# A two-part transformer forward pass on one core: another order of tiles in the mixing stage, earlier loads, squares one tile later

## The reference

```python
f = swiglu(rmsnorm(x, g1), w_gate, w_up, w_down);  x = x + 0.5 * rmsnorm(f, g2)
h = rmsnorm(x, mix_pre_g)
qa, ka, va, qb, kb, vb, gate_a, gate_b = split(h @ w_in)
ya = neighbourhood_attention(qa, ka, va, rpb) @ w_branch_a   # 8 heads, 8 rows x 16 columns, bias from rpb
yb = dilated_mixture(qb, kb, vb) @ w_branch_b
x = x + rmsnorm((sigmoid(gate_a) * ya + sigmoid(gate_b) * yb) @ w_out, g3)
...
# end of each hybrid layer: the per-layer embedding p, gated
x = x + sigmoid(rmsnorm(x, ple_g) @ w_ple_gate) * (p @ w_ple_proj)
# rope tables of the layers: cos and sin of positions * inv_freq
```

## Time and profile before

| | |
|---|---|
| median of 3 runs | 3201.22 us (3196.33 to 3205.59) |
| the profiled execution | 3208.67 us, its span 3206.9 us |
| mean granted TensorE clock | 0.988 |
| TensorE (PE) busy | 3094.5 us, 96% |
| VectorE (DVE) busy | 1714.4 us, 53% |
| ScalarE (ACT) busy | 1203.8 us, 38% |
| GpSimd (POOL) busy | 294.1 us, 9% |
| mean of one: L1705 cast, L1831 split, L1867 diagonal | 983, 1167, 689 ns |
| L1948 (mask), x6 | 1220 ns each |

### The profile page before, as it was taken

How to read it: one execution, slowest core, us unless ns; L and a number is a source line. 1 busy time by engine, 2 the same in 40 slices (tenths; PEclk the granted TensorE clock), 3 DMA queues, 4 the chain that set the end, 5 groups by cost and what they waited for, 6 DMA issues and landing times.

```text
span 3206.9 us, 40495 instructions
## 1 busy us (share of the span) xinstructions
PE 3094.5 (96%) x15386; PEld 2513.3 (78%) x15386; DVE 1714.4 (53%) x3078; ACT 1203.8 (38%) x2229; POOL 294.1 (9%) x351
## 2 busy tenths in 40 slices
PE   7999989999999999999999999999999999999997
PEld 5888777788788887777768888887877767888886
DVE  5653355346565426656656555435656665555435
ACT  3332325433433223645543323223545453332222
POOL 2000110001100012011001100012111001100002
PEclk9999999999999999999999999999999999999999
DMA  4323373225322333224216222333323314323332
GB/s 143 117 92 113 111 134 117 79 93 178 102 92 93 99 115 97 82 90 157 70 40 191 99 99 92 97 113 117 95 82 114 126 44 151 122 94 104 96 96 92
DMA packets 107569, 339.65 MB, mean 106 GB/s; under 512 B 16608, under 2 KB 17136, under 8 KB 107248
## 3 DMA queue, kind: packets, MB, share of 16 engines
q1 hardware_dynamic: 86384, 273.90, 26.9%
q0 software_dynamic: 20992, 63.15, 6.6%
HBM read 300.55 MB, written 27.52 MB: 102 GB/s over the span
## 4 chain that ended last, share of the span: by engine, by line
PE 83%; DVE 5%; ACT 5%; issue 3%; DMA 2%; POOL 1%; SPq 0%; POOLq 0%; DVEq 0%; ACTq 0%
PE bk L1537 24%; PE bk L1539 24%; PE bk L1538 24%; PE bk L1602 2%; PE bk L1624 2%; ACT t L1757 2%; PE bk L1610 2%; PE bk L1574 1%; PE bk L1576 1%; PE bk L1575 1%; ACT t L1705 1%; ACT t L1765 1%; DVE t L1831 1%; PE bk L1592 0%; PE bk L1587 0%
## 5 line engine op out<-in xcount | busy, mean ns | idle before, releaser
L1537 PE MATMUL bk<-t,t 128*128 128x512 f32 x3808 | 1499.1, 394 | 41.6 <-DVE t L1831 21.4
L1539 PE MATMUL bk<-t,t 128*128 128x512 f32 x3808 | 1482.3, 389 | 0.0
L1538 PE MATMUL bk<-t,t 128*128 128x512 f32 x3808 | 1481.3, 389 | 0.0
L1537 PEld LDWEIGHTS bk<-t,t 128*128 128x128 f32 x3808 | 719.6, 189 | 210.0 <-issue 51.2
L1831 DVE TENSOR_TENSOR t<-t,t 128x1024 fp32r<-128x1024 f32 (+3 forms) x540 | 620.3, 1167 | 421.1 <-ACT t L1705 420.6
L1538 PEld LDWEIGHTS bk<-t,t 128*128 128x128 f32 x3808 | 720.2, 189 | 147.6 <-issue 3.6
L1539 PEld LDWEIGHTS bk<-t,t 128*128 128x128 f32 x3808 | 719.4, 189 | 148.6
L1705 ACT CAST t<-t 128x1024 fp32r<-128x1024 f32 (+3 forms) x540 | 515.3, 983 | 227.8 <-PE bk L1539 116.3
L1757 ACT ACTIVATE t<-t,t 128x256 f32<-128x256 f32 (+3 forms) x336 | 174.1, 520 | 143.0 <-DVE t L1908 142.2
L1748 ACT CAST t<-t 128x512 fp32r<-128x512 f32 x88 | 54.7, 622 | 435.6 <-DVE t L1895 435.6
L2138 POOL TENSOR_TENSOR t<-t,t 128x512 f32<-128x512 f32 x65 | 86.9, 1337 | 1424.4 <-ACT t L1735 1423.6
(11 more groups left out here) (165 smaller groups left out, 2045.7 us busy)
## 6 DMA issues: line engine op xcount, KB each, us to landing
t<-in_f_g SPq DMA_DIRECT2D x88, 512.0 KB, 4.3
t<-in_f_u SPq DMA_DIRECT2D x88, 512.0 KB, 3.5
t<-in_f_d SPq DMA_DIRECT2D x64, 512.0 KB, 4.4
t<-in_gate SPq DMA_DIRECT2D x48, 512.0 KB, 3.7
gate_scratch<-t POOLq DMA_DIRECT2D x64, 256.0 KB, 2.3
t<-gate_scratch POOLq DMA_DIRECT2D x64, 256.0 KB, 3.9
t<-in_f_d SPq DMA_DIRECT2D x32, 384.0 KB, 3.2
t<-in_wo SPq DMA_DIRECT2D x24, 512.0 KB, 3.6
```

The costliest lines, as they stand in the source:

```text
L1537: pe.matmul(o, wh, xh, start=start, stop=False)
L1538: pe.matmul(o, wh, xl, start=False, stop=False)
L1539: return pe.matmul(o, wl, xh, start=False, stop=stop)
```

## The change

In the mixing stage the table loads wait for `ft[7]`, the last stored tile of the feed-forward, instead of `fr`. The q tiles come first and as one `dense4`, then three k tiles, the masks of heads 0 to 3, the values with their store and loads, the masks of heads 4 to 7, and the last k tile. The load of the positions is planned before `bias_tables`. In the embedding each tile's square is planned after the next tile's `dense`; in layer 0 the first three chunks are gained before the last tile's `gate`, the other five after it, and the last square after these.

```diff
--- before.py
+++ after.py
@@ -704,27 +704,32 @@
         va = [tile([128, 2, T], RA + (32 + 4 * w + 24 * (w > 1)) * K) for w in range(4)]
         BT = tile([128, 3, 8, 256], RA + 40 * K)
         bt_w = [self.load(BT[16 * r:16 * r + 16].rearrange("p w h k -> p (w h) k"),
-                          D["tables"][:, :, :, 7 - r:15 - r, :].rearrange("c w h a k -> c (w h) (a k)"), self.tables_t, fr)
+                          D["tables"][:, :, :, 7 - r:15 - r, :].rearrange("c w h a k -> c (w h) (a k)"), self.tables_t, ft[7])
                 for r in range(8)]
-        v_n = self.tokens_first("va", 512, 2, H, lambda t: vn[:, t, :], fr, by=lambda: (self.nv, self.nv_tok))
-        vst = self.load(D["values"].rearrange("(t p) c -> p t c", p=128), vn[:], v_n)
-        v_t = [[self.load(va[w][:, j, :],
-                          bass.AP(D["values"].tensor, (256 * j + WINDOWS[w]) * T, [[64 * T, 4], [T, 32], [1, T]]), fr, vst)
-                for j in range(2)] for w in range(4)]
         qt_, kt_ = [], []
         bt_ = {}
 
         def by_columns(a):
             return a.rearrange("p (r t c) -> p t r c", r=8, t=4)
 
+        for m, r in enumerate(self.dense4([("qka", m) for m in range(4)], H)):
+            qt_.append(self.evacuate(OB, *r, qa[:, m, :].rearrange("p (t r c) -> p t r c", t=4, r=8), fr, view=by_columns))
+        def masks(h0):
+            for kind in range(3):
+                n = self.step("biased", bt=BT[:, kind, h0:h0 + 4, :], window=kind, t=bt_w)
+                for i in range(h0, h0 + 4):
+                    bt_.setdefault(i, []).append((n, "d"))
+
         for m in range(4):
-            qt_.append(self.project("qka", m, H, qa[:, m, :].rearrange("p (t r c) -> p t r c", t=4, r=8), fr, view=by_columns))
-        for m in range(4):
+            if m == 3:
+                masks(0)
+                v_n = self.tokens_first("va", 512, 2, H, lambda t: vn[:, t, :], fr, by=lambda: (self.nv, self.nv_tok))
+                vst = self.load(D["values"].rearrange("(t p) c -> p t c", p=128), vn[:], v_n)
+                v_t = [[self.load(va[w][:, j, :],
+                                  bass.AP(D["values"].tensor, (256 * j + WINDOWS[w]) * T, [[64 * T, 4], [T, 32], [1, T]]),
+                                  fr, vst) for j in range(2)] for w in range(4)]
+                masks(4)
             kt_.append(self.project("qka", 4 + m, H, ka[:, m, :], fr))
-            for kind in range(3) if m % 2 == 0 else ():
-                n = self.step("biased", bt=BT[:, kind, 2 * m:2 * m + 4, :], window=kind, t=bt_w)
-                for i in range(2 * m, 2 * m + 4):
-                    bt_.setdefault(i, []).append((n, "d"))
         ob4 = {}
         oa_t = []
         na_us = []
@@ -913,8 +918,8 @@
         ki = tile([128, T], RA + 72 * K, I32)
         kf = tile([128, T], RA + 74 * K)
         r = [tile([128, T], RA + (76 + 2 * i) * K) for i in range(4)]
+        a = self.load(pi_[:], D["positions"].partition_broadcast(128), self.now())
         self.bias_tables()
-        a = self.load(pi_[:], D["positions"].partition_broadcast(128), self.now())
         yield
         done = []
         x = None
@@ -1444,7 +1449,12 @@
         fr = self.now()
         if L == 0:
             fetch, halves, product, store = self.embed(1, 4, RA, RA + 8 * K, fr, raw_at=RA + 16 * K)
-        new, back = [], {}
+        new, back, due, ht = [], {}, [], []
+
+        def squares():
+            for f in due:
+                f()
+            due.clear()
 
         def bring(m):
             if m < KC:
@@ -1459,8 +1469,12 @@
             tmp.give(io, (k, "o"))
             n = self.step("ple", m=m, s=s, t=[(k, "o"), xt[m]])
             tmp.give(i, (n, "d"))
-            self.acc_tok, r = self.square_in(self.xT[:, m, :], m == 0, (n, "d"), on="dve" if m == KC - 1 else "pool")
-            new.append([(n, "d"), r])
+            new.append([(n, "d")])
+
+            def square():
+                self.acc_tok, r = self.square_in(self.xT[:, m, :], m == 0, (n, "d"), on="dve" if m == KC - 1 else "pool")
+                new[m].append(r)
+            due.append(square)
 
         bring(0)
         bring(1)
@@ -1471,17 +1485,21 @@
                 fetch()
             if L == 0 and m == 5:
                 halves()
+            squares()
             if L == 0 and m == KC - 1:
                 for j in range(4):
                     product(j)
+                ht = [self.gained(9, c, list(new[c]), tg) for c in range(3)]
             if self.factor_due:
                 self.late.append(lambda a=(m, bg, gb, tg): gate(*a))
             else:
                 gate(m, bg, gb, tg)
         xt = new
-        ht = []
+        if L == 1:
+            squares()
         if L == 0:
-            ht = [self.gained(9, c, xt[c], tg) for c in range(KC)]
+            ht += [self.gained(9, c, list(xt[c]), tg) for c in range(3, KC)]
+            squares()
             xt = [[a, b] for a, b in zip(xt, ht)]
             for j in range(4):
                 store(j)
```

## The result

| | before | after |
|---|---|---|
| median | 3203.4 us (3196.33 to 3206.79, 4 runs) | 3166.58 us (3163.22 to 3167.88, 4 runs) |
| ratio, 95% interval | | 0.9882 [0.9871, 0.9893] |
| the profiled execution | 3208.67 us, span 3206.9 | 3163.22 us, span 3161.4 |
| mean granted TensorE clock | 0.988 | 0.996 |

A forecast was written before the change was run, and what follows sets the result against it. TensorE, busy 96%, bounds the kernel; only standing still and lower-clock stretches can go. 12.0 + 9.6 + 9.9 + 0.6 = 32.1 us off 3208.67 gives 3176.6; against the median 3201.22, 3169.1, range 3159 to 3186.

The forecast's parts named there:

- Positions: First feed-forward: the positions' load goes out sooner, VectorE's splits are done by 46.6, TensorE's stall goes; gain 12.0 us.
- the clock's share of it: First feed-forward: the lower clock behind the 9.07 us stall cost a further 2.9 us, part of the 12.0.
- Mixing: Mixing stage: q tiles first and tables earlier bring the first scores to 470.0 instead of 479.60; gain 9.6 us.
- a new wait of 3.9 us takes the place of the 8.28: Norm's second matmul (L1592): weights start when tables end, land at 433.3, so it cannot start before 436.5.
- The rival of shared queues: Mixing stage: the weight load shares engines from issue, the wait is 1 us, time 3166; chance 0.12.
- Values: Attention's first slot: value loads landed by E + 20.8, wanted at E + 22.3 (E: value tokens' end); cost 0.
- the rival of late values: Attention's first two slots wait as store or small loads meet weight loads; up to 18.6 us, 3187.7; chance 0.15.
- VectorE has over 4 us before each next split: Mixing stage: room for the masks, the same six operations (3.5 us for three), one group more behind the values.
- Embedding: Layer 0: late squares and three early gains remove TensorE's 7.88 us wait and 2.0 of lower clock; gain 9.9 us.
- the sum of the ring: Layer 0's embedding: ScalarE and VectorE take 5.9 us a tile against TensorE's 5.5; after, about 4.1 us.
- The rival of a ring that doesn't catch up: Layer 0's embedding: half of the wait stays, time 3174; chance 0.08.
- Tail: Layer 1's embedding: only the multiplication of 1.31 us beside GpSimd's addition may be freed to 0.69; gain 0.6 us.

The follow-up runs named there:

- u_pos: The changed kernel with the positions' load behind the bias-table loads again, nothing else undone; 3180.04 us, ratio to before 0.9919.
- u_mix: The changed kernel with the mixing stage in the old order, tables waiting for all work, positions and embedding as changed; 3182.03 us, ratio to before 0.9930.
- x_more: The changed kernel with eight more table loads of 128 KB, read by nobody, behind the eight; 3175.75 us, ratio to before 0.9909.
- m_vlast: The changed kernel with the values behind the last k tile instead of ahead of it, masks 4 to 7 behind them; 3174.28 us, ratio to before 0.9903.
- m_mask: The changed kernel with all six masks behind the last k tile instead of three before and three after the values; 3173.28 us, ratio to before 0.9905.
- u_emb: The changed kernel with the embedding as before (squares at once, gains last), positions and mixing stage as changed; 3179.61 us, ratio to before 0.9922.
- e_sq: The changed kernel with all eight gains behind the last gate in layer 0's embedding, squares still one tile late; 3165.26 us, ratio to before 0.9888.
- e_gain: The changed kernel with each square at once behind its tile's update, three gains still ahead of the last gate; 3180.58 us, ratio to before 0.9933.
- m_one: The changed kernel with the four q tiles made one after another in the same banks, not together chunk by chunk; 3182.19 us, ratio to before 0.9925.
- the changed kernel's second profile: Profile of the run "whole", the changed kernel measured again without further edits; 3167.33 us, ratio to before 0.9886.
- m_tab: The changed kernel with the table loads waiting for all work again, in the new order of tiles; 3182.72 us, ratio to before 0.9932.

## Why the forecast was right, and where it was not

**Positions: 12.0 forecast, 12.2 measured** between the profiles (12.7 by undoing, 10.2 in that run's trace). Right in each step: load at 34.4, VectorE there at 41.79 with the data in, splits done at 46.9 against 46.6 forecast, the lower clock gone with the stall. That the size fits within 0.2 us is in part luck, since the clock's share of it (2.9 forecast) was smaller in u_pos.

**Mixing: 9.6 forecast, 12.9 measured** between the profiles, 11.4 in the mixing column against u_mix. The sequence came as forecast: no wait for the squares, four q tiles at full pace, tables issued ahead, banks emptied in time, no wait for values. One term was mis-sized, and it is the whole difference.

The failed step is "a new wait of 3.9 us takes the place of the 8.28". It rests on a landing at 433.3, 34.55 us after the stage's first matmul; it was 31.2 (417.61 - 386.43). That the weights would come behind the tables was right, the sum over it was wrong: I let the load begin when the last table *lands* and gave it the whole 3.6 us from issue to landing. In the trace its first packet moves at 413.37, the tables' last ends at 415.43, while the last table's landing is told at 416.46, and the load is in at 417.61, when ScalarE takes it up:

```profile
417.63 1.05 ACT L1723 CAST t<-t 128x1024 fp32r<-128x1024 f32 x1 [9.37 <-DMA t<-in_va]
...
419.85 0.69 DVE L1885 TENSOR_TENSOR t<-t,t 128x512 f32<-128x512 f32 x1
```

That is 1.15 us behind the last table instead of 3.6. A weight load that had the queues to itself shows what is in such a time: issued at 440.61, its packets move from 441.57 to 443.83, and it landed at 444.18, so 2.3 of 3.6 us are packets. Here the load's start and the report of the tables' end (1.0 us) lay beside the other queue's packets. The tables too were quicker, 3.35 us apiece instead of 3.55. From landing to L1610 it was 3.08 us, as forecast (3.2). So L1610 came 34.26 us after the stage's first matmul, where 37.75 was forecast with the wait and 33.85 without, and from there to the first scores it was 33.7 us (33.5 forecast). The rival of shared queues (chance 0.12) named the right outcome, the weights in time and 3166 us, though its reason, a share from the issue on, did not hold: nothing moved for 4.7 us.

The Trainium skill (DMA: Bandwidth & Descriptors, Queues, rings and completion order) has each engine go round the queues that have work, one whole packet each. The traces agree with it in the later stretches (53.1% and 47.9% in x_more), and disagree for the first 4.7 to 10.9 us behind a queue with much issued, in which the new load gets nothing. Neither it nor my own reading (all tables first) fits alone, and in x_more, where queues that take turns from the issue on were to bring no wait, it was 6.27 us.

The wait removed, 9.9 us with fast matmuls ahead of it rather than 8.28 (u_mix), is no second error. The sum never added the 8.28: it set the new stage's first scores, at full pace, against the 479.60 of the trace, which holds both the slow matmuls and the wait. The 11.4 against u_mix are 1.5 less than the 12.9, because the profile before ran 7.2 us at the lower level behind its wait and u_mix 5.0 (1.1 us of time), and because the two profiles of the changed kernel differ by 0.4.

**Values: cost 0 forecast, 0 measured.** To spare were 2.5 us for the first slot (1.5 forecast: E + 20.8 against E + 22.3), since four loads were in at 468.69 against 471.22. The store took 5.2 us (4.8 to 5.2 in the runs with early tables). m_vlast shows that the rival of late values was real: issued 5.3 us later they cost 6.06 us of waiting. The masks, which I priced by "VectorE has over 4 us before each next split", are free in that place only (m_mask).

**Embedding: 9.9 forecast, 10.1 measured** (11.2 against u_emb between the two norms). That the early squares make the gate late is shown by e_sq and e_gain; the sum of the ring (5.9 us a tile against 5.5) was tested only through its result. The three early gains were in the forecast as if they mattered; they are a reserve. The rival of a ring that doesn't catch up falls: in e_sq VectorE waits for TensorE at the last gate.

**Tail: 0.6 forecast, 1.0 measured.** The multiplication that took 1.31 us takes 0.69 (at 3143.66), as forecast, and the squares undone bring it back (1.32 in u_emb). The wait ahead of the last norm is 4.37 us; with the squares undone it is 5.16 as before:

```profile
3146.61 1.84 PE L1605 MATMUL bk<-t,t 128*128 128x1 f32 x8 [4.37 <-DVE t L1873]
```

So the time came out 2.5 us below the forecast, and the gain, against the runs beside it, 4.7 us above it (36.8 against 32.1). By the profiles the mixing stage alone was 3.3 us better than forecast (12.9 - 9.6), the other parts 0.8 together; the rest is within the spread of the runs.

## What to carry to other kernels

- When two transfers follow each other, add only their packets' time. The time from issue to landing of an isolated load (3.6 us here, 2.3 of them packets) holds a start and a report that can overlap with what is ahead of it.
- A wait of an in-order engine for one late result can be filled only with work that eats its inputs no faster than they come: four tiles per chunk fill it, one tile per chunk turns it into seven small waits at the lower clock, at the same cost as the stall (m_one). And an engine that keeps falling behind in a ring with another is mended by moving the hand-over that nobody waits for (here the squares) by one turn, not by re-ordering what comes out at the end.
- A forecast of "no wait" that rests on a transfer is an edge. Say how far away it is: here 2 us more of tables made 1.9 us of waiting in one run, and 1 MB more 6.3.

## What the runs showed of the hardware

- The lower clock comes in stretches of 3.4 to 19 us: fourteen in the profile before (the first at 54.94), four in the one after. One near 1250 us and one near 2230 (1270 and 2263 before) are in every profile; the others come in some executions and not in others, also where the instructions are the same (six in the changed kernel's second profile). Of these, those behind a removed stall are the change's; the rest made most of 9.2 us between the two profiles, nearly as much as one of the three parts.
- A 1 MB store took 25.1 us behind tables and 5.2 us here without them; a 512 KB load 20.9 (before), 15.4 (x_more) and 9.0 us (changed) with tables issued ahead of it and still to come, and 8.3 in m_tab with one table ahead (the median of such loads on the page of the profile is 3.5).
- Eight small loads of the values, 256 KB each, took 6.7 to 15.2 us with one weight load among them (issued at 463.82). From 463.8 to 466 only their queue moved (97.2% of the engines), from 468 to 474 it had 35 to 58% and the weights' 31 to 63%.
